# Moving the attention blocks between the retention projections of a two-layer trunk: four, four, four, five, none

## The chip, the cores and the metric

The kernel runs on one core of one Trainium2 chip. The metric is device time in microseconds (us), the median of several runs. All data is float32.

## The reference

Two layers (`DEPTH = 2`) run over 512 latent tokens (4 tiles of 128) and 128 context tokens (1 tile), width 1024. The context tokens read only themselves, the latent tokens read cached context and all latent tokens. Cut to what matters here:

```
mod   = silu(c) @ w_mod[l] + b_mod[l]                    # 1024 x 6144, six shifts, scales and gates
h     = rms_norm(x) * (1 + sc1) + sh1
u, vg, ca, cg, rq, rk, rv, rgf, rgb, mla = split(h @ w_in)
y_a   = u * spatial_mix(rms_norm(vg))                    # chunked gating
y_b   = silu(layer_norm(conv31(ca * sigmoid(cg)))) @ w_pw
y_c   = silu(rgf) * norm(ret_fwd(rq, rk, rv)) + silu(rgb) * norm(ret_bwd(rq, rk, rv))
y_d   = softmax(q k^T / sqrt(96)) v                      # latent attention, 4 heads; q, k, v come from mla
x     = x + g1 * (concat(y_a, y_b, y_c, y_d) @ w_out)
x     = x + g2 * expert_choice_moe(rms_norm(x) * (1 + sc2) + sh2)   # 16 experts, 402 MB of weights over both layers
```

The attention (`y_d`) depends on the projection `mla` alone; the retention projections rq, rk, rv, rgf and rgb feed only `y_c`. So attention work may stand anywhere between them.

## The kernel before

Every engine runs a program written out by hand. TensorE (PE), ScalarE (ACT) and VectorE (DVE) each walk the same list `STEPS` (L87 to L95), issuing their part of each step, so one list sets the order on three engines at once. An engine never looks ahead past a wait.

**Dense part of a layer.** `in:<name>` multiplies the 640 tokens by a 256-column slice of `w_in` (`feature_major` L746 or `token_major` L758, 17.4 us of PE). `mod:a-b` computes 256-column units of `w_mod` for the two condition vectors: `mod_unit` (L689, matmuls at L701) and `mod_columns` (L704, matmuls at L710), which turns the rows of a unit into columns once ACT has copied them out. `conv_mean`, `mix`, `conv_var` and `conv_out` are the convolution and the gating; `ret_tables` makes decay tables on ACT and masks on DVE.

**Attention blocks.** There are 17 (`BLOCKS`): 16 of one head and one query tile with 640 keys, and a last one (block 16) for the context tile with all heads. `att:i` is software pipelined (`attend` L923): it issues the scores of block i (`scores` L868, lines L882, L883, or L880 for block 16), on every even i from 4 on the values of two earlier blocks (`weigh_values` L895, lines L918 and L920; step i takes pair (i-4)/2), and then the transposes of the probabilities of block i-2 (`turn_probs` L886, at the helper's line L721). For each block DVE reduces the row maxima (`score_max` L1824, lines L1830 and L1831), multiplies out finished values (`values_out` L1842) and copies turned probabilities (`probs_out` L1833, line L1840), in this order; ACT does exp (`softmax_exp` L1399, line L1410), copies the value scales (`scales_out` L1421) and the fifth turned chunk (`last_prob_out` L1413), in this order. `att_end` drains the pipeline (steps 17 to 20). Scores lie in the two PSUM banks of `wide`, turned probabilities in the two of `turned`, values and w_mod units in the two of `narrow`; each set is used in strict alternation in the order of `STEPS`, and a new job waits until the one before it in the same bank has been copied out.

**Weights.** Each unit of `w_mod`, `w_in` and `w_out` is a 1 MB load by the SP queue into one of three stream buffers (`NSTREAM = 3`). The list `UNITS` (L98) follows `STEPS`, and SP works through it in order:

```
UNITS: ..., rv, mod 15, rgf, mod 16, rgb, mod 17, mod 18, mod 19, mod 20, out 0, out 1, out 2, mod 21, ...
L581   last = UNITS[n - NSTREAM]
L582   (N if last[0] == "mod" else W).wait(sp, l, LAST_JOB[last])     # unit n-3 must be done
L587   sp.dma_start(stream[:, n % NSTREAM, :, 0:w], ...)
```

So the load of mod 19 is issued when the projection rgb is done, that of mod 20 when mod 17 is done, that of out 0 when mod 18 is done. PE waits for a unit in `next_unit` (L681).

**GpSimd (POOL)** has, in this part of a layer, two products in order: the queries times their decay (L2180, after rgb is done), then the keys times their decay (L2188, after block 16 has been scored and the masks are ready). `retention` on PE (L960) begins by waiting for the second.

**After it.** `rows_g1`, `router_bias`, `retention`, `out` (output projection), routing, and the mixture of experts, which streams 12 MB of weights for each of 16 experts.

The edited table and what reads it:

```
L90   for _n, _g in enumerate(["rq", "rk", "rv", "rgf", "rgb"]):
L91       STEPS += [f"in:{_g}", f"mod:{13 + _n}-{14 + _n}"]
L92       STEPS += {"rq": ["conv_mean", "mix"], "rk": ["conv_var"], "rv": ["conv_out"]}.get(_g, [])
L93       STEPS += [f"att:{_i}" for _i in range(_b, _b + BLOCKS_AFTER[_g])] + (["ret_tables"] if _g == "rv" else [])
L95   STEPS += ["mod:18-21", "att_end", "rows_g1", "router_bias", "retention", "out", ...]
```

Of the kernel before, what the change touches and what calls it, by code (L numbers as in the profile page):

```python
# [79 lines left out]
    return (i - VALUE_LAG) // 2 if i >= VALUE_LAG and i % 2 == 0 else None  # L80


BLOCKS_AFTER = {"rq": 3, "rk": 3, "rv": 3, "rgf": 3, "rgb": 5}

# [3 lines left out]
for _n, _g in enumerate(["rq", "rk", "rv", "rgf", "rgb"]):  # L90
    STEPS += [f"in:{_g}", f"mod:{13 + _n}-{14 + _n}"]  # L91
    STEPS += {"rq": ["conv_mean", "mix"], "rk": ["conv_var"], "rv": ["conv_out"]}.get(_g, [])  # L92
    STEPS += [f"att:{_i}" for _i in range(_b, _b + BLOCKS_AFTER[_g])] + (["ret_tables"] if _g == "rv" else [])  # L93
    _b += BLOCKS_AFTER[_g]
STEPS += ["mod:18-21", "att_end", "rows_g1", "router_bias", "retention", "out", "choose", "mod:21-24", "tables", "rows_g2"]  # L95
# [2225 lines left out]
```

How the kernel before makes its waits and increments, by code:

```python
    def claim(self, pe, l, job, e=0):  # L254
        pe.wait_ge(self.out_sem[self.buf(job)], START + self.half(l, job, e))
# [5 lines left out]
    def wait(self, eng, l, job, e=0):  # L262
        eng.wait_ge(self.done_sem, START + self.full(l, job, e) + 1)
# [5 lines left out]
    def taken(self, eng, l, job, e=0):  # L270
        eng.wait_ge(self.out_sem[self.buf(job)], START + self.half(l, job, e) + 1)
# [1 line left out]
    def layers_taken(self, eng, l):  # L274
        for s in self.out_sem:
            eng.wait_ge(s, START + l * (self.layer // 2) + self.ahead // 2)
# [1 line left out]
    def layers_done(self, eng, l):  # L279
        eng.wait_ge(self.done_sem, START + l * self.layer + self.ahead)
# [21 lines left out]
    def wait(self, n):  # L303
        self.eng.wait_ge(self.sem, self.base + n)
# [247 lines left out]
        @block.sync  # L552
# [3 lines left out]
                R.start(sp)  # L556
            for s in (s_silu, s_hm, s_ye, s_yep, s_rows_free):
                sp.sem_inc(s, START)
            sp.sem_inc(s_gu_used, KD)
            sp.dma_start(sT.rearrange("p k s -> p (k s)"), io["cond"]).then_inc(s_cond, 16)
            sp.dma_start(con_r, io["consts"]).then_inc(s_consts, 16)
            for t in range(NT):
                src = io["x_prompt"][0] if t == CTX else io["x_sample"][0, t * P:(t + 1) * P]
                sp.dma_start(x[:, t, :], src).then_inc(s_x[t], 16)
            sp.wait_ge(s_consts, 16)
            def load_head(l, u):
                slot = u - NSTREAM
                sp.wait_ge(s_gu_used, l * EXPERTS * KD + slot + 1)
                settle(sp)
                src = mod_h[bass.ds(l, 1), :, :, u * GW:(u + 1) * GW]
```

## Time and profile before

| | us |
|---|---|
| median of 3 runs (2109.42 to 2115.57) | 2111.23 |
| the profiled execution, its own time | 2113.24 |
| its span, first to last instruction | 2111.4 |
| PE busy, share of the span | 1960.2, 93% |
| DVE busy, ACT busy | 525.9, 471.9 |
| mean granted TensorE clock | 0.965 |

The span is one execution seen by the profiler; 1.8 us of its own time lie outside it. Busy PE is not PE at its peak: matmuls are pipelined and their ends are modelled. A row of the timeline gives the start, the length, the engine, the line, what is written and read, how many instructions were merged, and in brackets how long the engine had been idle before and what released it. The granted clock is 1.00 at 2.4 GHz and 0.50 at 1.2 GHz.

### The profile page before, as it was taken

The numbers are of one execution on the slowest core, as the hardware profiler recorded it, in microseconds if no ns is written. First come the engines' busy times: TensorE is split into PE (matmuls) and PEld (weight loads), VectorE is DVE, ScalarE is ACT, GpSimd is POOL, SyncE is SP. The second block draws the span as 40 slices with busy tenths as digits, with TensorE's granted clock in tenths as the row PEclk, the third lists the DMA queues.
The fourth block names the chain that finished last, engine by engine and source line by source line (L and its number), as shares of the span: only waits on it lengthen the run. The fifth ranks groups of instructions, "written<-read, shape, count | busy, mean of one in ns | idle before, by whom it ended". The sixth has DMA issues, their size and how long they took to land.

```text
span 2111.4 us, 36634 instructions
## 1 busy us (share of the span) xinstructions
PE 1960.2 (93%) x15008; PEld 1099.3 (52%) x15008; DVE 525.9 (25%) x1193; ACT 471.9 (22%) x1031; POOL 150.5 (7%) x124
## 2 busy tenths in 40 slices
PE   5999999994999999999979999989879999999995
PEld 3756677882434444343456656778634443434342
DVE  1257122624111110111121841245421111111112
ACT  2232233222212111111131223332321111212112
POOL 0000001000010110101000000000001101011110
PEclk9999899996999999999989999999889999999998
DMA  9213123147899999999943122225449999999997
GB/s 307 84 58 120 41 81 103 68 175 285 327 390 393 385 394 389 390 393 390 388 143 119 64 80 80 68 76 207 171 179 384 392 391 390 392 390 394 386 397 250
DMA packets 210040, 533.78 MB, mean 253 GB/s; under 512 B 17072, under 2 KB 99376, under 8 KB 209712
## 3 DMA queue, kind: packets, MB, share of 16 engines
q1 hardware_dynamic: 191824, 493.52, 61.5%
q0 software_dynamic: 12288, 23.07, 5.1%
q10 hardware_dynamic: 5856, 16.16, 1.9%
q8 instruction: 53, 0.87, 0.2%
q14 instruction: 19, 0.16, 0.0%
HBM read 506.59 MB, written 26.12 MB: 252 GB/s over the span
## 4 chain that ended last, share of the span: by engine, by line
PE 68%; DMA 14%; SPq 8%; DVE 4%; issue 3%; ACT 2%; ACTq 0%; DVEq 0%; POOLq 0%
PE wide L1169 13%; DMA ring<-w_up 12%; PE wide L765 9%; PE wide L755 8%; PE wide L1177 7%; SPq L595 7%; PE wide L1047 7%; PE narrow L1200 6%; PE wide L1213 3%; PE turned L721 2%; PE wide L882 1%; PE narrow L701 1%; PE narrow L1070 1%; PE narrow L918 1%; PE wide L1188 1%
## 5 line engine op out<-in xcount | busy, mean ns | idle before, releaser
L1169 PE MATMUL wide<-ring,ht 128*64 128x512 f32 x2048 | 454.9, 599 | 9.5 <-DMA ring<-w_up 4.9
L1169 PEld LDWEIGHTS wide<-ring,ht 128*64 128x64 f32 x2048 | 143.7, 138 | 305.2 <-issue 278.5
L1177 PE MATMUL wide<-ring,ht 128*32 128x256 f32 x4096 | 234.3, 380 | 0.0
L1200 PE MATMUL narrow<-ring,ht 128*64 128x512 f32 x1024 | 233.8, 598 | 0.0
L2034 DVE TENSOR_TENSOR ht<-ht,wide 128x512 f32<-128x512 f32 x64 | 35.5, 554 | 680.4 <-ACT ht L1625 460.0
L765 PE MATMUL wide<-stream,ht 128*128 128x256 f32 (+1 forms) x960 | 192.4, 362 | 3.5 <-DVE ht L1704 3.5
L1177 PEld LDWEIGHTS wide<-ring,ht 128*32 128x32 f32 x4096 | 126.5, 110 | 108.2 <-issue 31.3
L765 PEld LDWEIGHTS wide<-stream,ht 128*128 128x128 f32 x960 | 169.4, 190 | 24.2 <-issue 4.0
L755 PE MATMUL wide<-ht,stream 128*128 128x128 f32 (+1 forms) x640 | 178.4, 441 | 0.0
L1625 ACT ACTIVATE ht<-wide 128x512 f32<-128x512 f32 x32 | 19.1, 597 | 623.4 <-PE wide L1169 623.4
L2200 POOL DMA_INDIRECT moe_sums<-ht x64 | 99.5, 1554 | 773.9 <-DVE ht L2051 695.5
L755 PEld LDWEIGHTS wide<-ht,stream 128*128 128x128 f32 x640 | 99.1, 198 | 72.6 <-issue 72.6
L1200 PEld LDWEIGHTS narrow<-ring,ht 128*64 128x64 f32 x1024 | 67.8, 136 | 118.4 <-issue 115.8
L1213 PE MATMUL wide<-ring,ht 128*32 128x256 f32 x2048 | 117.1, 381 | 0.0
L1047 PE MATMUL wide<-stream,xn_yt 128*128 128x256 f32 x480 | 112.9, 391 | 1.6 <-ACT xn_yt L1377 1.6
L1315 ACT ACTIVATE ring<-wide 128x640 f32<-128x640 f32 (+7 forms) x56 | 40.2, 721 | 286.9 <-PE wide L765 156.2
L1047 PEld LDWEIGHTS wide<-stream,xn_yt 128*128 128x128 f32 x480 | 92.3, 196 | 14.6 <-ACT xn_yt L1315 2.0
L1779 DVE SCALAR_TENSOR_TENSOR ring<-ring,param_cols 128x670 f32<-128x670 f32 x120 | 99.4, 916 | 0.0
L1213 PEld LDWEIGHTS wide<-ring,ht 128*32 128x32 f32 x2048 | 63.3, 110 | 64.4 <-issue 26.0
L1617 ACT ACTIVATE ht<-turned,mod_cols,scale 128x64 f32<-128x64 f32 (+1 forms) x256 | 74.2, 394 | 9.1 <-PE turned L1160 8.7
L2051 DVE SCALAR_TENSOR_TENSOR ht<-narrow,ht 128x512 f32<-128x512 f32 x32 | 24.0, 750 | 183.7 <-PE narrow L1200 183.7
L2042 DVE TENSOR_SCALAR ht<-turned,scale,mod_cols 128x64 f32<-128x64 f32 (+1 forms) x256 | 60.9, 311 | 18.8 <-PE turned L1160 18.8
(263 smaller groups left out, 1576.8 us busy)
## 6 DMA issues: line engine op xcount, KB each, us to landing
ring<-w_gate SPq DMA_DIRECT2D x256, 512.0 KB, 12.5
ring<-w_up SPq DMA_DIRECT2D x256, 512.0 KB, 14.1
ring<-w_down SPq DMA_DIRECT2D x128, 1024.0 KB, 19.7
stream<-w_mod SPq DMA_DIRECT2D x38, 1024.0 KB, 5.5
stream<-w_in SPq DMA_DIRECT2D x20, 1024.0 KB, 7.4
ring<-w_mod SPq DMA_DIRECT2D x10, 1024.0 KB, 12.0
stream<-w_out SPq DMA_DIRECT2D x6, 1024.0 KB, 5.9
moe_sums<-x ACTq DMA_DIRECT2D x10, 512.0 KB, 6.8
```

What stands on the lines that cost most here:

```text
L595: sp.dma_start(ring[:, k, i, :], src.rearrange("l e p n -> (l e p) n")).then_inc(s_slot[k], 16)
L755: ins = mm(o[:, lo:hi], w[:, k, c * P:(c + 1) * P], hT[:, k, lo:hi], start=(k == 0), stop=(k == KD - 1))
L765: ins = mm(o[:, n * width:(n + 1) * width], src[:, k, t * P:(t + 1) * P], w[:, k, 0:width], start=(k == 0), stop=(k == KD - 1))
L1047: ins = mm(bank(W, f"o.{t}")[:, u * GW:(u + 1) * GW], yT[:, k, t * P:(t + 1) * P], out_weights[u][:, k, :], start=(u % 2 == 0 and k == OTH ...
L1169: ins = mm(psW[h * 64:(h + 1) * 64, 0, w * HALFW:(w + 1) * HALFW], xT[:, k, 0:CAPS], ring[:, k, w, h * HALFW:(h + 1) * HALFW], start=(k == ...
L1177: ins = mm(psW[q * STRIP:(q + 1) * STRIP, 1, w * QW:(w + 1) * QW], xT[:, k, CAPS:SLOTS], ring[:, k, w, q * QW:(q + 1) * QW], start=(k == 0 ...
L1200: ins = mm(psN[c * 64:(c + 1) * 64, 0, :], hmT[:, j, h_ * 64:(h_ + 1) * 64], ring[:, KD + k // 2, k % 2, c * HALFW:(c + 1) * HALFW], start ...
L1213: ins = mm(psW[q * STRIP:(q + 1) * STRIP, 1, HALFW:HALFW + QW], hmpT[:, j, q_ * STRIP:(q_ + 1) * STRIP], ring[:, KD + k // 2, k % 2, q * Q ...
L1617: ins = A(xT[:, k, lo:lo + n], bank(T, job)[:, k * GROWS + lo:k * GROWS + lo + n], ACT.Identity, scale=A2[:, k, s_:s_ + 1], bias=modT[:, 3 ...
L1779: ins = V.scalar_tensor_tensor(cacc[:, c, :], src, w[:, c, k:k + 1], cacc[:, c, :], ALU.mult, ALU.add)
L2042: ins = V.tensor_scalar(xT[:, 4 + k, lo:lo + n], bank(T, job)[:, k * GROWS + lo:k * GROWS + lo + n], A2[:, 4 + k, s_:s_ + 1], modT[:, 3 * ...
L2200: Q.indirect_dma_start(dst, bass.IndirectOffsetOnAxis(tables[:, j, e:e + 1], 0), src, None, compute_op=ALU.add).then_inc(s_added, 16)
```

## The change

```
-BLOCKS_AFTER = {"rq": 3, "rk": 3, "rv": 3, "rgf": 3, "rgb": 5}
+BLOCKS_AFTER = {"rq": 4, "rk": 4, "rv": 4, "rgf": 5, "rgb": 0}
```

It is the whole diff. Blocks 0 to 3 now stand behind rq, 4 to 7 behind rk, 8 to 11 behind rv, 12 to 16 behind rgf and none behind rgb. Behind rgb the list goes on at once with mod 17 and the three units of `mod:18-21`, then `att_end`. The order of the weight units does not change, nor does any instruction.

## Rows read from the trace of the kernel before

**Rows 1.** The page, part 4: the chain that ended last, by engine
```profile
PE 68%; DMA 14%; SPq 8%; DVE 4%; issue 3%; ACT 2%; ACTq 0%; DVEq 0%; POOLq 0%
```
**Rows 2.** Timeline of PE, layer 0, behind rq and in the retention; last, the second layer
```profile
211.21 2.08 PE L882 MATMUL wide<-ring 96*128 96x512 f32 x2 [1.94 <-ACT ring L1410]
...
391.55 3.34 PE L1011 MATMUL turned<-ring 128*128 128x64 f32 x16 [2.50 <-DVE ring L1873]
...
1248.84 2.08 PE L882 MATMUL wide<-ring 96*128 96x512 f32 x2 [1.94 <-ACT ring L1410]
```
**Rows 3.** Timeline of PE, layer 0, the blocks behind rk
```profile
242.28 1.91 PE L882 MATMUL wide<-ring 96*128 96x512 f32 x2
...
248.24 2.17 PE L918 MATMUL narrow<-ring 128*64 128x128 f32 x20 [1.69 <-issue]
...
253.55 17.43 PE L765 MATMUL wide<-stream,ht 128*128 128x256 f32 x80
```
**Rows 4.** Busy time by stretch, with granted clock (0.50), DMA share, GB/s
```profile
211.00:217.80 6.80, 6.59 (x25) 5.56 (x26) 1.79 (x5) 2.09 (x7) 0.00 (x0) 0.50 0.01 2
248.50:251.90 3.40, 3.40 (x30) 3.07 (x27) 0.36 (x2) 0.70 (x3) 0.00 (x0) 0.50 0.00 0
391.90:398.70 6.80, 6.80 (x25) 5.99 (x25) 6.56 (x15) 2.46 (x6) 0.00 (x0) 0.50 0.39 123
```
**Rows 5.** Timeline of ACT: first exp behind rk, first exp behind rgb
```profile
247.09 0.79 ACT L1410 ACTIVATE ring<-wide,stats 128x640 f32<-128x640 f32 x1
...
332.90 0.80 ACT L1410 ACTIVATE ring<-wide,stats 128x640 f32<-128x640 f32 x1 [0.52 <-DVE stats L1831]
```
**Rows 6.** Timeline of PE: first block and next projection, behind rv and behind rgf
```profile
276.79 1.02 PE L882 MATMUL wide<-ring 96*128 96x512 f32 x2
...
285.57 17.43 PE L765 MATMUL wide<-stream,ht 128*128 128x256 f32 x80
...
304.40 1.10 PE L882 MATMUL wide<-ring 96*128 96x512 f32 x2
...
311.65 17.43 PE L765 MATMUL wide<-stream,ht 128*128 128x256 f32 x80
```
**Rows 7.** Timeline of PE: five blocks behind rgb (12, 16), the w_mod units, retention's start
```profile
330.49 1.10 PE L882 MATMUL wide<-ring 96*128 96x512 f32 x2
...
340.98 1.06 PE L880 MATMUL wide<-ring 96*128 96x128 f32 x8
...
344.99 1.07 PE L701 MATMUL narrow<-stream,cond_cols 128*32 128x256 f32 x16
...
346.91 0.58 PE L710 MATMUL narrow<-const_cols,mod_rows 128*128 128x2 f32 x4 [0.85 <-DVE xn_yt L1847]
...
350.09 1.23 PE L710 MATMUL narrow<-const_cols,mod_rows 128*128 128x2 f32 x8
351.18 0.74 PE L721 MATMUL turned<-const_cols,ring 128*128 128x128 f32 x5
...
362.14 2.68 PE L974 MATMUL narrow<-ring 128*64 128x64 f32 x64
```
**Rows 8.** SP's loads, issue to landing: mod 19 (at 329.1), mod 20 (330.2), slowest pair (181.3, 182.3)
```profile
stream<-w_mod SPq DMA_DIRECT2D x1, 1024.0 KB, 5.2
...
stream<-w_mod SPq DMA_DIRECT2D x1, 1024.0 KB, 7.7
...
DMA to landing us min/median/max: 7.3/8.1/9.0
```
**Rows 9.** Timeline of POOL and of DVE around block 16, layer 0
```profile
329.18 4.67 POOL L2180 TENSOR_TENSOR ht<-ring 128x1024 f32<-128x1024 f32 x2 [259.11 <-PE wide L765]
342.29 4.65 POOL L2188 TENSOR_TENSOR ring<-ring,stats 128x1280 f32<-128x1280 f32 x2 [8.45 <-PE wide L880]
...
341.49 0.15 DVE L1831 TENSOR_SCALAR stats<-stats 128x1 f32<-128x1 f32 x1
...
342.95 1.71 DVE L1831 TENSOR_SCALAR stats<-stats 128x4 f32<-128x4 f32 x1
```

## The prediction

> **What bounds the kernel now.** I began with the chain that ended last: PE carries 68% of it and loads 14% [rows 1]. The loads belong to the experts, which the change doesn't touch and which start only when the dense part of the layer has ended; so any time won or lost before them moves the end by as much. Next I read PE's timeline between the gating and the retention. The reader should see there that PE works nearly without a break: each projection is one solid row of 17.4 us, and idle time shows only inside groups of attention blocks, where a score or a transpose waits for an exp or a copy [rows 2, 3, 6, 7]. So PE's order bounds this part, and a change of order can gain only by removing such waits or loses by making new ones. Third, the clock: after a wait of 1.94 us, and after one of 2.50 us, the granted clock stood at 0.50, that is 1.2 GHz, for 6.8 us, after one of 1.69 us for 3.4 us [rows 2 to 4]. PE is busy through these stretches and does half the work, so a wait costs itself plus 3.4 us or 1.7 us. The second layer repeats the first 1037.6 us later [rows 2]; I price one layer and double it.
>
> **The change, group by group (one layer).** No instruction is added or removed, so I compare lengths of groups.
>
> Behind rq: a fourth block adds a score and a transpose. Its price is that of a fourth block to an even-started group: 10.49 less 8.78, both below, 1.7 us. The half clock that follows the 1.94 us wait is there as before; it now covers the new block instead of the start of rk [rows 2, 4]. Its bank and its exp are free by then. **+1.7.**
>
> Convolution part behind rk: unmoved in order, 0. It runs at a clock that changes in its neighbourhood, and a half-clock stretch that falls on it or off it is worth 1.7 us either way.
>
> Behind rk: now blocks 4 to 7 instead of 3 to 5, which took 242.28 to 253.55, 11.3 us [rows 3]. The shape (even start, two value pairs) is that of blocks 12 to 15: 330.49 to 340.98, 10.5 us [rows 7]. But there the first exp starts 2.4 us after the first score, and here 4.8 us after it, since ACT first does the two silus of the convolution and a table load [rows 3, 5, 7]. In the new order PE's own work hides until the second transpose: that needs the first one's bank, which DVE frees only after the value product, which waits for ACT's scales behind that exp. So the whole group is 2.4 us later: 12.9. PE then waits some 2.7 us at one place, nearest to the rows with 6.8 us of half clock: +3.4, of which about 1.1 fills waits that the group has anyway, so 2.3. Total 15.2. **+3.9** (ends: 12.9, +1.6, with no clock fall; 16.3, +5.0, with all of it).
>
> Behind rv: blocks 8 to 11, even start, 10.5 us against 8.8 (276.79 to 285.57) [rows 6, 7]. **+1.7.**
>
> Behind rgf and rgb: blocks 12 to 16 take 14.5 us (330.49 to 344.99) in either place; the odd-started group of 7.25 us (304.40 to 311.65) goes [rows 6, 7]. **-7.25.** So far the regrouping costs about nothing: 1.7 + 3.9 + 1.7 - 7.25 = 0.05.
>
> Tail: this is where I expect the loss. Let T be the end of rgb (329.0 before). Before, mod 17 took 1.5 us, then came 14.5 us of blocks, under which the loads of mod 19 and mod 20 landed, then mod 18 to 20 took 344.99 to 351.18, 6.2 us [rows 7]: 7.7 us without the blocks. Now nothing stands between. The loads are issued by the same rule, when rgb and mod 17 are done: T+0.1 and T+1.2. They took 5.2 and 7.7 us to land [rows 8], so T+5.3 and T+8.9. PE does mod 17 and mod 18 with their columns (1.0 and 0.5 us each) until T+2.95, waits 2.4 us, does mod 19 until T+6.9, waits 2.0 us, does mod 20 (1.0) and two sets of columns (1.1) [rows 7] until T+11.0. **+3.3.** With the slowest pair, 7.3 and 9.0 us [rows 8], mod 20 starts at T+10.2: +4.6. What these waits hide: ACT and DVE finish block 16 under rgb instead, so the 0.85 us that mod 18's columns waited for them goes [rows 7]; it is in the 6.2 already.
>
> Clock in the tail: two waits of 2.4 and 2.0 us within 6 us. The nearest rows give 6.8 us of half clock, 3.4 us of lost work; the drain of attention that comes next waits for DVE by itself, and slower PE fills part of that (1.1 us, an estimate). I take **+2.3** (ends 0 and 5.1, one more such stretch). The Trainium skill (TensorE: Matmul & The Clock Gate, the two states) ties the fall to 1.2 GHz to an idle stretch longer than either of these waits. By that rule this term and the clock part behind rk would be 0, and the sum 2.3 + 2.3 us smaller in each layer. The rows of this trace fall after 1.94 and 1.69 us [rows 2 to 4], so the sum stays as it is.
>
> POOL: its two products, 4.7 us each, now follow one another right behind rgb, since the first waits for rgb and stands in front of the second: until T+9.5. Retention on PE waits for them, but comes after the tail, the drain of attention, g1 rows and router bias: before, 351.18 to 362.14, so T+22 [rows 7]. Hidden, 12 us to spare. DVE's scaling of the maxima of block 16 took 1.71 us beside POOL, that of block 15 0.15 us without it [rows 9]. The Trainium skill (SBUF — State Buffer, two separate sides) says that one port pair is held exclusively by DVE or GpSimd for a whole instruction, and the trace's 1.71 us agrees. Now POOL is still when block 16 passes, and DVE has nothing in T to T+9.5 but is back for the drain at T+11.5: no cost, 2 us to spare.
>
> Out 0 to 2 are loaded behind mod 18, 19 and 20; the last lands by T+18, before T+22. 0.
>
> **Sum:** 1.7 + 3.9 + 1.7 - 7.25 + 3.3 + 2.3 = 5.65 a layer, 11.3 for both. The profiled execution took 2113.2, so 2124.5 by its own count; the median of the runs shown is 2.0 lower, and I predict for the median: 2111.2 + 11.3 = 2122.5.
>
> **Rivals.**
> (1) The waits come but the clock falls little: behind rk 12.9 and nothing in the tail. 1.7 + 1.6 + 1.7 - 7.25 + 3.3 = 1.05 a layer, 2113.3; with one of the two falls 2117. That is the page's rule too. Against it stand three rows of half clock after shorter or equal waits; for it, that the wait of 0.85 us at 346.9 did nothing to PE's pace [rows 7]. 0.22.
> (2) Not slower: the block that moves behind rq gives the group behind rk so much finished work that the half clock there (before 245.1, and 248.5 to 251.9) disappears and the exp's delay hides: 10.5 us for the group and 1.7 less in the convolution part. The place is the second transpose behind rk; it decides if PE waits there less than about 1.5 us. 1.7 - 1.7 - 0.8 + 1.7 - 7.25 + 3.3 = -3.05 a layer, 2105. It needs the tail's clock to hold also. For it: 4 blocks behind rk carry more PE work than 3. Against: the chain exp, scales, value product, copy is longer than the one before. 0.04.
> (3) Worse: loads as slow as the slowest pair (+1.3), one more half-clock stretch in the tail (5.1 instead of 2.3) and all of it behind rk (+1.1): 10.85 a layer, 2133. For it: the pair at 181.3 was slow with nothing else in flight. 0.14.
> The forecast itself, 2117.6 to 2130, has 0.60. That the change doesn't do what it says can be left out: one table makes the order of all engines.
>
> **How the numbers follow.** A measurement of this kernel tells about 0.3%, 6.3 us. Slower by more: the forecast, nearly all of (3), and a few hundredths of (1): 0.76. Within: the rest of (1) and half of (2), with some of the forecast's low edge: 0.21. Faster: 0.03. Range: 2113 (rival 1 without clock) to 2131 (most of rival 3) leaves out under 0.2.
>
> **What would show it.** In the new trace: PE idle before L701 twice behind rgb, released by the loads of w_mod, 2.4 and 2.0 us; mod 20's columns ending near 11.0 us after rgb; granted clock 0.50 in the stretch behind it; behind rk one wait of about 2.7 us before a transpose; groups of 10.5 behind rv and 14.5 behind rgf; POOL's second product directly behind its first. I am wrong if the loads of mod 19 and mod 20 are waited for less than 3 us together, or if the group behind rk takes under 12 us.

## The result, and the profile after

The changed kernel takes 2124.43 us (median of 16 runs, 2118.24 to 2129.81) against 2109.47 us (16 runs, 2106.59 to 2118.86): ratio 1.0071, 95% interval 1.006 to 1.0082, about 15 us slower. The forecast was 2122.5 us in a range of 2113 to 2131, 11.3 us slower. The profiled execution has a span of 2123.7 us, 12.3 us over that of before. That is less than 15, because the profiled execution of before was a long one (2113.24 us, 3.8 over its median) and that of the change nearly a usual one (2125.51 us, 1.1 over).

First the group of w_mod matmuls in the table of groups (busy time, mean ns | idle before them, what ended it); before, the same group had 17.6 us of idle time before it, 17.3 of it ended by loads. The chain's shares moved by one point at most (DMA 15%, ACT 1%, against 14% and 2% in [rows 1]):

```profile
L701 PE MATMUL narrow<-stream,cond_cols 128*32 128x256 f32 x608 | 48.4, 448 | 24.0 <-DMA stream<-w_mod 23.6
```

A group's idle time says that PE waits 6.4 us more for w_mod units, but not where. PE's timeline of layer 0 says it: from the end of rgb to the drain of attention, and the start of g1 rows and of the retention. It answers to [rows 7]:

```profile
341.12 1.07 PE L701 MATMUL narrow<-stream,cond_cols 128*32 128x256 f32 x16
342.12 0.61 PE L710 MATMUL narrow<-const_cols,mod_rows 128*128 128x2 f32 x4
342.79 1.07 PE L701 MATMUL narrow<-stream,cond_cols 128*32 128x256 f32 x16
343.79 0.61 PE L710 MATMUL narrow<-const_cols,mod_rows 128*128 128x2 f32 x4
346.69 1.07 PE L701 MATMUL narrow<-stream,cond_cols 128*32 128x256 f32 x16 [2.30 <-DMA stream<-w_mod]
347.69 0.61 PE L710 MATMUL narrow<-const_cols,mod_rows 128*128 128x2 f32 x4
349.69 1.93 PE L701 MATMUL narrow<-stream,cond_cols 128*32 128x256 f32 x16 [1.40 <-DMA stream<-w_mod]
351.56 1.87 PE L710 MATMUL narrow<-const_cols,mod_rows 128*128 128x2 f32 x8
353.29 1.31 PE L721 MATMUL turned<-const_cols,ring 128*128 128x128 f32 x5
...
360.64 3.84 PE L957 MATMUL wide<-const_cols,mod_cols 128*128 128x128 f32 x32
...
366.19 2.68 PE L974 MATMUL narrow<-ring 128*64 128x64 f32 x64
```

The reader is to see two things. The brackets: mod 19 and mod 20 each wait for their load. And the lengths: the last w_mod unit takes 1.93 us instead of 1.07, its columns 1.87 instead of 1.23, the transposes 1.31 instead of 0.74. That is half clock (a granted clock of 0.50), and the busy times by stretch confirm it (columns as in [rows 4]; both half-clock stretches of the two tails):

```profile
348.30:358.40 10.10, 8.13 (x55) 6.13 (x56) 0.69 (x1) 2.18 (x9) 2.24 (x1) 0.50 1.03 326
1389.40:1406.30 16.90, 14.78 (x101) 10.94 (x94) 2.18 (x5) 2.95 (x11) 3.64 (x2) 0.50 0.71 224
```

In layer 1 the same two waits are 2.19 and 0.77 us, and half clock lasts 16.9 us. From rgb's end to g1 rows PE takes 19.5 us (341.12 to 360.64) in layer 0 and 21.0 us in layer 1. Before, it was 27.6 us with 14.5 us of blocks inside, so 13.1 without.

The groups of blocks. Behind rk, where one wait stands, in layer 0 and then in layer 1; it answers to [rows 3]:

```profile
244.07 1.91 PE L882 MATMUL wide<-ring 96*128 96x512 f32 x2
...
251.09 0.74 PE L721 MATMUL turned<-const_cols,ring 128*128 128x128 f32 x5 [1.65 <-issue]
...
256.78 17.43 PE L765 MATMUL wide<-stream,ht 128*128 128x256 f32 x80
...
1293.49 0.74 PE L721 MATMUL turned<-const_cols,ring 128*128 128x128 f32 x5 [0.69 <-issue]
```

And behind rv and rgf, which answer to [rows 6, 7]:

```profile
280.02 1.02 PE L882 MATMUL wide<-ring 96*128 96x512 f32 x2
...
290.51 17.43 PE L765 MATMUL wide<-stream,ht 128*128 128x256 f32 x80
...
309.35 1.10 PE L882 MATMUL wide<-ring 96*128 96x512 f32 x2
...
323.76 17.43 PE L765 MATMUL wide<-stream,ht 128*128 128x256 f32 x80
```

These are 10.5 us behind rv and 14.4 us behind rgf. Where the 12.3 us of the span arose, by stages of PE's timeline (start of a stage to start of the next, before and after in each layer):

| stage, us | before, both layers | after, layer 0 | after, layer 1 |
|---|---|---|---|
| blocks behind rq, then rk up to `conv_var` | 31.0 | 29.9 | 32.7 |
| `conv_var` | 4.4 | 6.2 | 5.2 |
| blocks behind rk | 11.3 | 12.7 | 12.7 |
| blocks behind rv | 8.8 | 10.5 | 10.6 |
| blocks behind rgf, with mod 16 | 8.7 | 15.9 | 15.9 |
| rgb's end to g1 rows | 27.6 | 19.5 | 21.0 |
| g1 rows to retention | 5.5 | 5.5 | 6.4 |
| from the first block to the retention, all stages | 155.3 | 158.3 | 162.5 |

So 3.0 and 7.2 us, and the other 2.1 us lie before the first block of layer 0 and in the experts of layer 1, where the change doesn't reach. One profile of each kernel doesn't carry more than this. The runs of before alone spread over 16 us, and the spread goes with the mean granted clock of the run: over 28 runs of the kernel before, made beside the experiments, time rises by 1.8 us for each 0.001 that the clock is lower (2118.8 and 2119.1 us at 0.961, 2103.0 to 2105.6 us at 0.969). The changed kernel's mean clock is 0.9591 over its 16 runs, that of before 0.9663 in those 28. At that slope the difference alone would be 13 us. That is too much to put down to the clock, since half clock in the tail lies partly over waits, where it costs nothing; the filled run below separates the two. But it says where to look. Read in slices of half a microsecond, the profile of before holds some 151 us of half clock and that of the change some 176, 25 more, and the two tails of the change alone hold 27. The question is what brings it there.

### The profile page after: what moved, and what is told of

The parts are those of the page before. It is cut to its first block, busy times and chain, and to the rows that moved or that the text cites. A ratio compares the mean times of both kernels' runs of the same rounds, so it can differ in the third digit from the quotient of the medians.

```text
span 2123.7 us, 36632 instructions
## 1 busy us (share of the span) xinstructions
PE 1968.8 (93%) x15008; PEld 1105.2 (52%) x15008; DVE 522.3 (25%) x1193; ACT 468.9 (22%) x1029; POOL 150.4 (7%) x124
## 4 chain that ended last, share of the span: by engine, by line
PE 68%; DMA 15%; SPq 8%; DVE 4%; issue 3%; ACT 1%; ACTq 0%; DVEq 0%; POOLq 0%
PE wide L1169 13%; DMA ring<-w_up 12%; PE wide L765 9%; PE wide L755 8%; PE wide L1177 7%; SPq L595 7%; PE wide L1047 7%; PE narrow L1200 6%; PE wide L1213 3%; PE turned L721 2%; PE wide L882 1%; PE narrow L701 1%; PE narrow L918 1%; PE narrow L1070 1%; PE wide L1188 1%
## 5 line engine op out<-in xcount | busy, mean ns | idle before, releaser
L1625 ACT ACTIVATE ht<-wide 128x512 f32<-128x512 f32 x32 | 19.1, 597 | 623.2 <-PE wide L1169 623.2
L701 PE MATMUL narrow<-stream,cond_cols 128*32 128x256 f32 x608 | 48.4, 448 | 24.0 <-DMA stream<-w_mod 23.6
## 6 DMA issues: line engine op xcount, KB each, us to landing
ring<-w_gate SPq DMA_DIRECT2D x256, 512.0 KB, 12.7
```

The costliest lines, as they stand in the source:

```text
L701: ins = mm(psN[q * STRIP:(q + 1) * STRIP, N.buf(job), 0:GW], sT[:, k, :], w[:, k, :], start=(k < 4), stop=(k >= 4))
```

## The experiments

Theory A: the tail is the whole loss, by the two uncovered loads and the half clock that these waits bring. Rivals: B, the regrouping in front costs; D, the half clock has nothing to do with the waits; and others named below. Each ratio is to the kernel before, run beside it on the same chip; in the first four experiments its median was 2108.66 us. A ratio isn't the quotient of the two medians; the two differ by up to 0.0013, inside the intervals given.

**The regrouping alone.**

```
-BLOCKS_AFTER = {"rq": 3, "rk": 3, "rv": 3, "rgf": 3, "rgb": 5}
+BLOCKS_AFTER = {"rq": 4, "rk": 4, "rv": 4, "rgf": 0, "rgb": 5}
```

> Blocks 4, 4, 4, none behind rgf, 5 behind rgb: the regrouping of the change with the tail of the kernel before. Theory A (the whole loss lies in the tail: two waits for loads and the half clock behind them): behind rgb the rows are those of before, no wait for a load of w_mod; groups of 8.2, 12.7, 10.5 and 14.5 us, the 7.25 us group gone, so 1.6 to 3.5 us won in each layer: 2104 to 2108 against 2109.5, clearly below the changed kernel. Rival B (the regrouping itself costs: the convolution part and the group behind rk at half clock, the extra block behind rq): 2113 or more, that is over a third of the 15 us loss stays.

2113.22 us, ratio 1.0026 (1.0012 to 1.0041). The tail is that of before to 0.1 us, as expected, and the group of three is gone. But the kernel isn't faster, it is a little slower. A missed, since it wanted a gain, and the bound of B, 2113 or more, is just reached: the regrouping does seem to cost something, 5.5 us by the ratio. Its mean clock is 0.963 over 12 runs against 0.9663.

**The tail alone.**

```
+BLOCKS_AFTER = {"rq": 3, "rk": 3, "rv": 3, "rgf": 8, "rgb": 0}
```

> Blocks 3, 3, 3, 8, none: the tail of the change with the first three groups of before. Theory A: both load waits appear behind rgb (about 2.3 and 1.4 us) and the tail from rgb's end to the retention is 6 to 9 us longer in each layer; the odd group of 3 and the group of 5 merge at no gain: 2122 to 2127. Rival B: 2109 to 2113, since the groups behind rq and rk are unchanged.

2120.61 us, ratio 1.0057 (1.0036 to 1.0077). Both waits stand behind rgb, in PE's timeline:

```profile
351.01 1.07 PE L701 MATMUL narrow<-stream,cond_cols 128*32 128x256 f32 x16 [2.17 <-DMA stream<-w_mod]
352.01 0.66 PE L710 MATMUL narrow<-const_cols,mod_rows 128*128 128x2 f32 x4
354.72 1.94 PE L701 MATMUL narrow<-stream,cond_cols 128*32 128x256 f32 x16 [2.04 <-DMA stream<-w_mod]
```

Rgb's end to g1 rows is 19.8 us in both layers, at a granted clock of 0.74. The median is 1.4 us below what A expected and 7.6 above the top of B's range. The tail by itself makes most of the loss; B is out as its main cause, not as a part of it.

**The drain in front of the w_mod units.** The changed kernel with

```
-STEPS += ["mod:18-21", "att_end", "rows_g1", ...
+STEPS += ["att_end", "mod:18-21", "rows_g1", ...
```

> The changed kernel with the drain of attention moved in front of the three w_mod units, so that 5.4 us of PE work lie under the two loads. Theory A: the wait for mod 19 is gone and that for mod 20 under 1 us, no half clock behind rgb, all of the 15 us back and the 3 to 5 us of the regrouping on top: 2104 to 2110. Rival C (the wait only moves: the three w_out units are now loaded 5 us later and PE waits for them in the retention): a wait of 2 us or more before the first L1047 there, 2112 to 2118.

2107.68 us, ratio 0.9985 (0.9968 to 1.0002). The loss is gone, but a gain over before isn't resolved. PE's timeline in layer 0:

```profile
349.38 1.07 PE L701 MATMUL narrow<-stream,cond_cols 128*32 128x256 f32 x16
350.56 0.58 PE L710 MATMUL narrow<-const_cols,mod_rows 128*128 128x2 f32 x4
351.06 1.07 PE L701 MATMUL narrow<-stream,cond_cols 128*32 128x256 f32 x16
352.06 0.61 PE L710 MATMUL narrow<-const_cols,mod_rows 128*128 128x2 f32 x4
352.73 1.07 PE L701 MATMUL narrow<-stream,cond_cols 128*32 128x256 f32 x16
...
364.90 2.83 PE L1047 MATMUL wide<-stream,xn_yt 128*128 128x256 f32 x12 [0.58 <-DMA stream<-w_out]
```

No unit waits for a load any more, all three run at full clock, and rgb's end to g1 rows is 12.3 us, 0.8 less than before without its blocks. Of rival C only a little shows: the wait for w_out is 0.58 us, not 2, and in layer 1 there is none.

**The waits filled with matmuls.** In `mod_unit` of the changed kernel, ahead of the wait for the load. Nothing reads what they write.

```
+                if u in (19, 20):
+                    N.claim(pe, l, job)
+                    for _ in range({19: 9, 20: 5}[u]):
+                        mm(psN[:, N.buf(job), GW:2 * GW], ident, con("expo")[:, 0:GW], start=True, stop=True)
```

> The changed kernel with matmuls that nothing reads in front of mod 19 (9 of them, 1.96 us) and mod 20 (5, 1.1 us): the loads land as late as before, but PE is busy meanwhile. It separates the waits from the clock. Theory A: the granted clock stays at 1.00 behind rgb, mod 20 still begins 8.5 us after rgb, the tail shrinks by the 3.4 and 5.7 us that are lost to half clock: 2114 to 2118. Rival D (the half clock behind rgb doesn't come from the waits, as a rule that wants a longer idle stretch would have it): half clock stays, 2122 to 2127. Rival E (waits alone are the loss): the same 2122 to 2127, with the clock at 1.00.

2119.91 us, ratio 1.0045 (1.0027 to 1.0063), outside all three expectations, because the filling was mis-sized: each of these matmuls shows as two instructions, 0.46 us together, so 9 and 5 of them took 4.15 and 2.43 us and themselves put off the units. The clock was 1.00 in both tails, and the mean clock of the 9 runs 0.9668 against 0.9663: here the late units, put off a little further, make the kernel slower at the clock of before. Again with 4 and 2:

> As the run with filled waits, whose 9 and 5 matmuls took 4.15 and 2.43 us, about 0.46 us each and so longer than the waits; here 4 in front of mod 19 (1.8 us) and 2 in front of mod 20 (0.9 us), inside the waits of 2.3 and 1.4 us. Theory A: no half clock behind rgb, mod 20 begins 8.5 us after rgb, rgb's end to g1 rows 16.2 us instead of 19.5 and 21.0: 2114 to 2118. The same median as the changed kernel (2122 or more) would say that the clock costs nothing there.

2119.06 us against 2109.97 us, ratio 1.003 (1.0015 to 1.0045), 1 us above what was expected. Now the loads are what ends the wait again; PE's timeline (the filling matmuls are at L696, and lines behind them are 4 higher):

```profile
346.03 1.99 PE L696 MATMUL narrow<-const_cols 128*128 128x256 f32 x8
348.31 1.07 PE L705 MATMUL narrow<-stream,cond_cols 128*32 128x256 f32 x16 [0.28 <-DMA stream<-w_mod]
...
349.88 1.13 PE L696 MATMUL narrow<-const_cols 128*128 128x256 f32 x4
351.82 1.07 PE L705 MATMUL narrow<-stream,cond_cols 128*32 128x256 f32 x16 [0.81 <-DMA stream<-w_mod]
```

The two tails by stretch, clock 1.00 in both:

```profile
342.80:359.30 16.50, 13.77 (x146) 9.48 (x145) 1.64 (x4) 4.54 (x17) 9.27 (x4) 1.00 0.98 314
1384.00:1400.60 16.60, 13.73 (x146) 9.45 (x145) 1.65 (x4) 4.54 (x17) 9.27 (x4) 1.00 0.98 313
```

The tail takes 16.5 and 16.7 us, against 19.5 and 21.0 in the change and 13.1 before. The loads land no sooner than in the change, so 3.5 us a layer is the price of the late loads and 3.0 to 4.3 us a layer (with 0.8 us more on g1 rows in layer 1) that of the half clock. Work that nobody needs makes the kernel faster: the ratio is 1.003, against 1.0071 and, when the change was run again, 1.0063 (1.004 to 1.0085). These were not run side by side, and the last interval touches that of the filled run, so the price of the clock rests on the lengths of the tails more than on the medians. Rival D falls with the clock of 1.00 in the tails of both filled runs, rival E with the tails that are 3.0 and 4.3 us shorter.

**Two blocks behind rgb.**

```
+BLOCKS_AFTER = {"rq": 4, "rk": 4, "rv": 4, "rgf": 3, "rgb": 2}
```

> Blocks 4, 4, 4, 3 and 2. Two blocks (15 and 16, about 5.5 us of PE) lie over the loads of mod 19 and mod 20, which land 5.3 and 8.9 us after rgb. Theory A: neither is waited for, no half clock behind rgb, and the time is that of the regrouping alone, 2110 to 2115, against 2124 for the change. Rival (the tail is slow for another reason than uncovered loads, for instance POOL's two products or the drain): 2118 or more.

2111.16 us against 2109.97 us, ratio 0.9994 (0.9976 to 1.0013). Both tails are at 1.00, and neither load is waited for:

```profile
341.23 1.07 PE L701 MATMUL narrow<-stream,cond_cols 128*32 128x256 f32 x16
343.45 0.58 PE L710 MATMUL narrow<-const_cols,mod_rows 128*128 128x2 f32 x4 [1.15 <-DVE xn_yt L1847]
343.95 1.07 PE L701 MATMUL narrow<-stream,cond_cols 128*32 128x256 f32 x16
...
345.62 1.07 PE L701 MATMUL narrow<-stream,cond_cols 128*32 128x256 f32 x16
```

Mod 18's columns wait for the values of block 16, a wait that the change had removed, but it is 1.15 us long and takes no clock with it. 5.7 us of blocks (335.5 to 341.2) are cover enough. This run has the change's first three groups, and no loss that the interval can tell.

**Fewer blocks behind rq, and behind rk.** These ask whether waits in the front part can be had back as well. In turn 2, 4, 4, 2, 5; 2, 4, 4, 7, 0 with the drain first; 2, 2, 4, 4, 5.

```
+BLOCKS_AFTER = {"rq": 2, "rk": 4, "rv": 4, "rgf": 2, "rgb": 5}
```

> Blocks 2, 4, 4, 2 and 5: the tail of before, and only two blocks behind rq, so that the third score, which waits 1.94 us for an exp behind the gating's work on DVE, comes after rk. Theory A (waits of 1.7 us and more cost themselves and half clock behind them): that wait and up to 6.8 us of half clock go in each layer: 2100 to 2105. Rival F (it moves behind rk, where ACT's silus and table load hold the exp back until 4.8 us after the convolution part, and the third score there waits 2 us or more and takes the clock with it): 2107 to 2112.

2107.45 us, ratio 0.9979 (0.9961 to 0.9996), in the range of rival F.

```
+BLOCKS_AFTER = {"rq": 2, "rk": 4, "rv": 4, "rgf": 7, "rgb": 0}
+STEPS += ["att_end", "mod:18-21", "rows_g1", ...
```

> Blocks 2, 4, 4, 7 and none, with the drain in front of the three w_mod units, as in the drain run (2107.7). Theory A: both gains add up, no half clock behind rq and behind rgb: 2098 to 2104, which beats both kernels clearly. Rival F as in the run with two blocks behind rq: 2106 to 2110.

2107.39 us, ratio 0.9984 (0.9967 to 1.0002), in the range of rival F.

```
+BLOCKS_AFTER = {"rq": 2, "rk": 2, "rv": 4, "rgf": 4, "rgb": 5}
```

> Blocks 2, 2, 4, 4 and 5: only two blocks behind rq and two behind rk, so no third score stands behind either of the two stages where DVE or ACT is late, and all later groups start even. Theory A: no wait over 1 us behind rq or rk, groups of 4.5, about 4, 10.5, 10.5 and 14.5 us, 44 a layer against 49.5 before, with less half clock on top: 2098 to 2104, ratio to before 0.995 to 0.998, under the 0.998 of two behind rq alone. Rival G (the half clock behind the convolution part comes from that part itself and stays, and DVE's delay only moves to the first score behind rv): 2105 to 2109.

2108.33 us against 2110.37 us, ratio 0.9998 (0.9984 to 1.0012), in the range of rival G. The first again:

> Blocks 2, 4, 4, 2 and 5 once more, the best ratio so far (0.9979, interval 0.9961 to 0.9996). If the gain is real, 0.997 to 0.999 with 1 outside the interval or at its edge; if it was where the clock's falls lay, 0.999 to 1.001, since two behind rq and two behind rk, which should have been better still, gave 0.9998.

2107.84 us against 2108.78 us, ratio 0.9995 (0.9984 to 1.0005). The wait of 1.94 us behind rq isn't gone in any of them. It has moved by one step: with two blocks there, the first matmuls of the projection rk wait, 2.02 or 2.03 us, for the same exp, and 3.4 us of half clock follow that wait in four of the eight layers. PE's timeline of 2, 4, 4, 2, 5 shows it at 212.60, then the score at half clock at 240.44, and a wait of 1.23 us behind rk:

```profile
212.60 19.02 PE L755 MATMUL wide<-ht,stream 128*128 128x128 f32 x64 [2.03 <-ACT ring L1410]
...
240.44 1.91 PE L882 MATMUL wide<-ring 96*128 96x512 f32 x2
...
246.44 0.30 PE L721 MATMUL turned<-const_cols,ring 128*128 128x128 f32 x1 [1.23 <-ACT ring L1315]
```

Theory A's 5 to 10 us of gain didn't come, nor did they add up. But these three versions don't test whether removing that wait would pay, since none removes it; and rival F, though its numbers came, looked for the wait behind rk, where it is 1.2 us and not 2. No version beats the kernel before by more than these comparisons tell.

**The regrouping and the change once more, side by side.**

> The regrouping alone (4, 4, 4, none, 5) once more. It ran at 1.0026 of before, while 4, 4, 4, 3, 2, which has the same first three groups, ran at 0.9994. If the regrouping has a cost of its own: 1.002 to 1.004 again, at a mean clock 0.002 or more under before. If the first result was where the clock's falls happened to lie: 0.999 to 1.001.

> The changed kernel again, on the same chip and beside the same runs of before as the regrouping alone: 1.006 to 1.008, mean clock about 0.959 against 0.966. The part of the loss that belongs to the regrouping is then the ratio of the regrouping run over this one, in one comparison.

The regrouping alone: 2113.88 us, 1.0016 (1.0002 to 1.003), mean clock 0.9628 against 0.9658. The ratio lies between the two that were expected, the clock on the side of a cost. The change, 6 runs: 2121.19 us, 1.0063 (1.004 to 1.0085), mean clock 0.9595. So the first result of the regrouping was hardly an accident, and about 0.2% is its share in this form, which leaves about 0.5% for the tail (1.0063 less 1.0016), beside 1.0057 for the tail alone. Whether 4, 4, 4, 3, 2 (0.9994, to 1.0013) escapes it isn't resolved. Stage by stage the regrouping's profile is no longer than that of before up to the retention: 152.0 and 154.9 us, again 153.8 and 153.5 us, against 155.3. The clock of the repeated run, by stretch (rgb's end to the retention, and then the retention and the output projection), followed by the same two stretches of the kernel before:

```profile
328.90:362.00 33.10, 28.73 (x307) 21.99 (x306) 12.55 (x29) 14.89 (x46) 9.31 (x4) 1.00 0.50 159
362.00:402.00 40.00, 36.19 (x303) 31.78 (x303) 25.27 (x63) 11.12 (x27) 0.00 (x0) 0.87 0.10 31
```

```profile
329.00:362.10 33.10, 28.72 (x307) 21.99 (x306) 12.56 (x29) 14.89 (x46) 9.31 (x4) 1.00 0.49 159
362.10:402.00 39.90, 36.09 (x310) 31.81 (x311) 26.98 (x67) 11.37 (x27) 0.00 (x0) 0.91 0.10 31
```

The lower clock here is one more short half-clock stretch in the retention, whose order the change doesn't touch. Whether such falls follow from when the front part ends, or only from where this execution happened to stand, one profile a run can't tell. Over the whole profile half clock is some 155 us in the first run of the regrouping and 162 in the second, against 151 before, and 121 and 118 us of it, against 111, lie outside the stretches from the first block to the output projection, so mostly where the change doesn't reach. That part of the loss stays open.

The second profile of the change has the same tails, 19.1 and 20.7 us with 10 and 17 us of half clock, and it corrects two readings of the first. In layer 1 only mod 19 is waited for:

```profile
1387.83 1.93 PE L701 MATMUL narrow<-stream,cond_cols 128*32 128x256 f32 x16 [2.34 <-DMA stream<-w_mod]
1389.69 1.01 PE L710 MATMUL narrow<-const_cols,mod_rows 128*128 128x2 f32 x4
1390.84 1.94 PE L701 MATMUL narrow<-stream,cond_cols 128*32 128x256 f32 x16
```

One wait of 2.34 us stands before these 17 us, so a second wait isn't needed for them. And behind rk the waits are 1.68 and 1.91 us, 3.4 us of half clock follows each, and the group takes 14.1 us in both layers, where the first profile, with waits of 1.65 and 0.69 us and no new fall, has 12.7.

## Why the prediction was right

The sign, the range and the place were right: slower, by 15.0 us where 11.3 was forecast, in the tail behind rgb by two uncovered loads and the half clock behind them. How near the number came is in part luck. In the profile the priced stages grew by 3.0 and 7.2 us, against 5.65 forecast for each: behind rk 2.5 us too much was priced and behind rq in layer 0 2.8, in the tail's clock 0.7 and 2.8 too little and in the convolution part 1.8 and 0.8. (In the second profile they grew by 5.1 and 7.8 us, 160.4 and 163.1 against 155.3.) And by medians the regrouping, priced at 0.05 us a layer, cost 0.16 to 0.26% in its two comparisons, 3.4 to 5.5 us, for a reason that stays open; the tail alone cost 0.57%, 12 us, where 3.3 + 2.3 a layer, 11.2 us, was forecast. Step by step:

- **Behind rq, +1.7.** Layer 1 has exactly this (31.0 to 32.7). In layer 0 the half clock after the 1.93 us wait did not come at all, and the stage is 1.1 us shorter than before. That the fall "is there as before" holds on average at best.
- **Convolution part, 0, ends 1.7 either way.** It took 1.8 and 0.8 us more, by half clock in it. The bound was needed, and 0.1 us too narrow for layer 0.
- **Behind rk, +3.9.** Measured +1.4 twice. The mechanism stands: the second transpose waits for DVE's copy behind the exp. But it waits 1.65 and 0.69 us, not 2.7, because the half clock of the convolution part reaches into the group (its first score takes 1.91 us, not 1.10) and slower work fills the wait; and no further fall followed in these two layers, where I had taken 2.3 us. In the second profile it did follow, and the group took 14.1 us, +2.8. Together with the line before it, the region behind rk came to +3.2 and +2.2 against my 3.9.
- **Behind rv, +1.7, rgf and rgb, -7.25.** Measured +1.7 and +1.8, and 14.4 against 14.5 us for the five blocks. Lengths of groups of the same parity carried over to 0.1 us.
- **The tail's loads, +3.3.** Loads landed 5.4 and 7.3 us after issue (forecast 5.2 and 7.7), PE waited 2.30 and 1.40 us (2.4 and 2.0), and mod 20 began 8.6 us after rgb in layer 0 (8.9) and 9.0 in layer 1. Its price with the clock held is 3.5 us, by the filled run.
- **The tail's clock, +2.3.** The largest miss: 3.0 us in layer 0 and about 5.1 in layer 1 (4.3 and 0.8). Half clock lasted 10 and 17 us, where I took the 6.8 us of the nearest rows. The length isn't explained: two waits stand close together here, but the second profile has 17 us behind a single wait of 2.34 us. The upper end I gave, 5.1, is what layer 1 took, though one more stretch of 3.4 us on top of 2.3 would have made it 5.7.
- **The rule on the clock.** All six tails with uncovered loads (two profiles of the change, one of the tail alone) fall to half clock after a first wait of 2.17 to 2.34 us, and none of the filled ones does, though their loads are as late: so the wait brought it. The rule of the Trainium skill (TensorE: Matmul & The Clock Gate, the two states), by which this term would have been 0, doesn't hold here. Outside the tail the length of a wait doesn't decide by itself: 1.94 us was followed by half clock before and 1.93 us behind rq in the change was not, nor was 1.65 us behind rk, while 1.68 us was.
- **POOL, 0.** Its two products ran back to back, 341.28 to 350.54, and DVE's next operation came at 354.4, so the spare time was there. The scaling for block 16, now with POOL still, took 0.17 us, in the same form that took 1.71 us beside POOL [rows 9]:

```profile
321.81 0.17 DVE L1831 TENSOR_SCALAR stats<-stats 128x4 f32<-128x4 f32 x1
```

- **Out 0 to 2, 0.** The retention began on time in the change. With the drain in front it is no longer free: 0.58 us.

Rival 1, that the clock would hold, was wrong in the tail. Rival 2 (not slower) had its place behind rk. Its deciding wait came out on both sides of the 1.5 us that I named (1.65 and 0.69 us), but the half clock in the convolution part did not go. What the forecast did not see is how much one execution differs from the next: it built on one profile, in which both layers show the same falls. In the run of the tail alone, whose order up to rv is that of before, the stages from the first block to rv take 46.7 us in layer 0, as before, and 42.5 us in layer 1.

## What to carry to other kernels

When work is moved away from in front of a run of short steps that each need a load, compute when each load is issued by the buffer rule and what PE still has to do until it lands; a profile of before gave both to about 0.6 us in layer 0. Price a new wait of PE of about 2 us with the clock and without it, as a range: here half clock followed such a wait often but not always, in the tail always, and lasted 3.4 to 17 us. When a wait seems gone, look whether the next matmuls on the same bank have it now. Moving the drain of attention, work that was there anyway, over the loads gave all of it back.

## What the runs showed of the hardware

The same kernel's time goes with its mean granted clock, 1.8 to 2.1 us for 0.001 in the four sets of runs of before, and that mean differs from run to run (0.961 to 0.970), so two profiles may differ by several us without any difference in the code. Short work that nobody reads, 1.99 and 1.13 us of matmuls inside two waits, kept the granted clock at 1.00 through a tail that without it ran 10 to 17 us at 0.50. And of two loads issued 1 us apart by one queue the second landed 2.9 us after the first (342.3 + 7.3 against 341.3 + 5.4); it took 7.3 us with the load of out 0 issued 1.7 us behind it, and 7.7 us before, where out 0 came 16 us later [rows 8], so no delay by the load behind it shows.
